# A two-layer decoder trunk on 8 cores: the mixer norm's weight applied behind the spatial product, and steps of the recurrent layer moved between engines

## The reference, cut to what matters

```
def rg_lru(xc, h0, w_a, b_a, w_x, b_x, lam):
    r = sigmoid(block_diag_linear(xc, w_a, b_a))
    i = sigmoid(block_diag_linear(xc, w_x, b_x))
    log_a = -LRU_C * r * softplus(-lam)
    a = exp(log_a)
    mult = sqrt(-expm1(2.0 * log_a))
    bterm = mult * (i * xf)
    ...
def lru_mixer(...):
    gate, xb = split(xn @ w_in)
    xc, conv_tail = causal_dwconv(xb, conv_past, conv_w, conv_b)
    h, h_last = rg_lru(xc, ...)
    y = (gelu(gate) * h) @ w_out
def gmlp_mixer(xn, w_in, ln_g, ln_b, w_s, b_s, w_out):
    u, v = split(gelu(xn @ w_in))
    v = layernorm(v, ln_g, ln_b)
    ws = where(mask, w_s, 0)              # (G, CHUNK, CHUNK), 8 groups, chunks of 128
    s = einsum('gts,bcsgd->bctgd', ws, vp) + b_s
    y = (u * s) @ w_out                   # v is returned too, for the samples
```

## Time and profile before

| | us |
|---|---|
| three runs: median | 1739.13 |
| three runs: lowest and highest | 1738.28 and 2018.64 |
| the profiled execution | 1739.17 |
| its span on the slowest core (core 5) | 1737.6 |
| spans of the 8 cores | 1728.8 to 1737.6 |
| mean granted clock of TensorE, by core | 0.988 to 0.992 |

### The profile page before, as it was taken

The page is one execution under the profiler, slowest core; times in us unless marked ns, Lnnn a source line. Parts: engine busy times, 40 slices in busy tenths (PEclk is TensorE's granted clock), DMA queues, the critical chain, the costliest instruction groups (busy, mean ns, idle before and its releaser), DMA issues.

```text
span 1737.6 us, 35664 instructions; the slowest of 8 cores (1728.8 to 1737.6 us)
## 1 busy us (share of the span) xinstructions
PE 1650.4 (95%) x10879; PEld 1052.6 (61%) x10879; DVE 1267.9 (73%) x2604; ACT 950.3 (55%) x1918; POOL 643.8 (37%) x1101
## 2 busy tenths in 40 slices
PE   5899989999999999999988999999999999999996
PEld 2566655666666666666544556656666666666655
DVE  4676666987767676777767877888776777677786
ACT  4877779644444444466655453864444444565756
POOL 1444447432111111136866654722111111254543
PEclk9899999999999999999999999999999999999998
DMA  8710040073212121210094000133440404001112
GB/s 158 169 56 2 2 79 1 3 133 69 44 31 48 27 49 25 43 20 1 11 164 79 2 1 1 27 63 66 78 73 2 74 1 74 2 5 38 39 48 101
DMA packets 24074, 82.96 MB, mean 48 GB/s; under 512 B 1872, under 2 KB 15504, under 8 KB 18128
## 3 DMA queue, kind: packets, MB, share of 16 engines
q0 software_dynamic: 9712, 59.16, 19.9%
q1 hardware_dynamic: 13200, 20.32, 3.5%
q10 hardware_dynamic: 976, 1.21, 0.3%
HBM read 129.81 MB, written 10.03 MB: 80 GB/s over the span
## 4 chain that ended last, share of the span: by engine, by line
PE 76%; DVE 7%; issue 5%; ACT 5%; POOL 4%; DMA 2%; DVEq 0%; ACTq 0%; POOLq 0%; SPq 0%
PE PS L583 76%; DVE SB L567 3%; POOL SB L542 3%; DVE SB L542 3%; ACT SB L531 2%; ACT L531 1%; DMA SB<-xT 1%; DVE SB L558 1%; ACT SB L572 1%; ACT PS L531 1%; DMA SB<-lru_w_a 0%; DMA SB<-lru_w_x_in 0%; POOL SB L558 0%; DVE SB L1363 0%; POOL SB L556 0%
## 5 line engine op out<-in xcount | busy, mean ns | idle before, releaser
L583 PE MATMUL PS<-SB 128*128 128x352 bf16 (+5 forms) x10879 | 1650.4, 313 | 79.3 <-ACT SB L531 36.2
L583 PEld LDWEIGHTS PS<-SB 128*128 128x128 bf16 x10879 | 1052.6, 98 | 676.9 <-issue 124.3
L567 DVE SCALAR_TENSOR_TENSOR SB<-SB 128x352 f32<-128x352 f32 (+1 forms) x708 | 398.0, 582 | 219.4 <-ACT SB L572 192.4
L542 POOL TENSOR_TENSOR SB<-SB 128x352 f32<-128x352 f32 (+12 forms) x457 | 437.1, 971 | 304.0 <-PE PS L583 103.2
L542 DVE TENSOR_TENSOR SB<-SB,PS 128x352 f32<-128x352 f32 (+3 forms) x960 | 458.2, 513 | 71.4 <-PE PS L583 54.0
L531 ACT ACTIVATE SB<-PS,SB 128x352 f32<-128x352 f32 (+1 forms) x432 | 256.7, 616 | 349.9 <-PE PS L583 336.1
L531 ACT ACTIVATE SB<-SB 128x352 f32<-128x352 f32 (+6 forms) x646 | 309.5, 505 | 236.5 <-DVE SB L567 136.4
L574 POOL COPY SB<-SB 128x2 f32<-128x2 f32 (+2 forms) x456 | 142.5, 317 | 623.3 <-ACT SB L572 446.9
L567 DVE SCALAR_TENSOR_TENSOR SB<-SB,PS 128x352 bf16<-128x352 f32 (+6 forms) x448 | 222.9, 546 | 92.6 <-ACT PS L531 50.1
L531 ACT ACT_TABLE_LOAD x111 | 142.4, 1283 | 56.3 <-PE PS L583 37.8
L572 ACT ACTIVATE SB<-PS 128x352 f32<-128x352 f32 (+7 forms) x408 | 159.8, 408 | 23.6 <-PE PS L583 12.2
(11 more groups left out here) (27 smaller groups left out, 55.8 us busy)
## 6 DMA issues: line engine op xcount, KB each, us to landing
SB<-ffn_w_up POOLq DMA_DIRECT2D x24, 1024.0 KB, 11.6
SB<-ffn_w_down POOLq DMA_DIRECT2D x12, 1024.0 KB, 9.1
SB<-xT SPq DMA_DIRECT2D x10, 704.0 KB, 9.0
yT<-SB SPq DMA_DIRECT2D x10, 704.0 KB, 3.3
SB<-ple_w_gate POOLq DMA_DIRECT2D x2, 2048.0 KB, 19.1
SB<-gm_w_in POOLq DMA_DIRECT2D x2, 2048.0 KB, 21.4
SB<-lru_w_x_in POOLq DMA_DIRECT2D x4, 512.0 KB, 10.5
SB<-lru_w_g_in POOLq DMA_DIRECT2D x2, 1024.0 KB, 19.8
```

The lines of the kernel that those rows point to most:

```text
L542: emit(eng, lambda e: e.tensor_tensor(out=out.ap, in0=a.ap, in1=b.ap, op=op), R=[a, b], W=[out], cost=c)
L567: emit("dve", lambda e: e.scalar_tensor_tensor(out=out.ap, in0=a.ap, scalar=sa, in1=b.ap, op0=op0, op1=op1), R=rr, W=[out], cost=c)
L583: emit("pe", lambda e: e.matmul(ps.ap, lhsT=lhsT.ap, rhs=rhs.ap, start=start, stop=stop), R=[lhsT, rhs], W=[ps], cost=max(0.05, 0.000427 * ...
```

## The change

The norm's weight and bias no longer touch v on its way to the spatial product. As the spatial product works on tokens and the weight stands per feature, the weight is applied behind it, as a scalar per partition in the same instruction that adds the position bias. The bias b of a feature becomes b times the row sum of the masked matrix; g_prep1 forms that with two products a group, of b in two bf16 parts, and adds it to bsB. Only the samples' block, whose v is an output, still gets both, in f32. The normalisation now writes the bf16 block itself.

In the recurrent layer: the load of lru_w_a waits for half a tile of x; tile 5's copies out of PSUM go from ACT to Vector; squares and clamps of tile 0 and of every other block of tile 5 go from Pool to Vector; tile 5's gates stand behind the exponentials and its roots behind the gates; two of the gates come with the output groups and six behind them. In layer 0's channel mixer the norms of tiles 2 to 5 form half of their squares on ACT, and lru_tail must be done before tile 3. `vecs` has 8 more columns.

```diff
+        lnbT = T(mem, [D], F32, off=ggate.off + 512)
+        lnbh = T(mem, [D], BF16, off=ggate.off + 4608)
+        lnbl = T(mem, [D], BF16, off=ggate.off + 6656)
...
-        load("pool", lw_a.all(), kp(w_la, KC), K("lwa"), hblock(0, 8, TN, TN))
+        load("pool", lw_a.all(), kp(w_la, KC), K("lwa"), hblock(0, 4, TN, TN))
...
-            cp(xb.v((3, 3 + npr)), sub(ps, 0, npr), eng="act")
+            cp(xb.v((3, 3 + npr)), sub(ps, 0, npr), eng="dve" if ns else "act")
             if ns:
-                cp(OLC.v(c, 0), sub(ps, npr - 3, npr), eng="act")
+                cp(OLC.v(c, 0), sub(ps, npr - 3, npr))
                 p3 = s4(sub(ps, npr, n))
                 cp(xs.v(None, (0, 3)), lcs.v(c), eng="pool")
-                cp(xs.v(None, (3, 7)), p3, eng="act")
-                cp(OLC.v(c, (1, 17)), V(p3.ap[:, :, 1:4], p3.bufs), eng="act")
+                cp(xs.v(None, (3, 7)), p3)
+                cp(OLC.v(c, (1, 17)), V(p3.ap[:, :, 1:4], p3.bufs))
...
-        def gate_group(ti, c):
+        def gate_group(ti, c, behind="sqrt"):
...
-            keep("gelu", act(gg[(ti + 1) % 2][c].v((0, n)), ps, AF.Gelu_apprx_tanh, order=phase("sqrt")))
+            keep("gelu", act(gg[(ti + 1) % 2][c].v((0, n)), ps, AF.Gelu_apprx_tanh, order=phase(behind)))
...
-            tt(m, a, a, ALU.mult, eng="pool")
-            ts(m, m, 1.0, ALU.min, 0.0, ALU.max, eng="pool")
+            eng = "dve" if ti == 0 or ti == 5 and c % 2 else "pool"
+            tt(m, a, a, ALU.mult, eng=eng)
+            ts(m, m, 1.0, ALU.min, 0.0, ALU.max, eng=eng)
...
-            keep("sqrt", act(m, m, AF.Sqrt, bias=0.25, scale=-0.25, order=phase("exp", "rstd")))
+            keep("sqrt", act(m, m, AF.Sqrt, bias=0.25, scale=-0.25, order=phase("gelu") if ti == 5 else phase("exp", "rstd")))
...
         for c in range(KC):
-            gate_group(5, c)
+            if c < 2:
+                gate_group(5, c, "exp")
             out_group(4, c)
+            tick()
+        for c in range(2, KC):
+            gate_group(5, c, "exp")
             tick()
...
-        bg.append(("xn2", xn_norm("nf0", 2, None, "pool", False)))
+        bg.append(("xn2", xn_norm("nf0", 2, None, ["act", "pool"] * 4, False)))
+        bg.append(("xn3", xn_norm("nf0", 3, None, ["act", "pool"] * 4, False)))
         bg.append(("tail", lru_tail()))
-        bg.append(("xn3", xn_norm("nf0", 3, None, "pool", False)))
-        bg.append(("xn4", xn_norm("nf0", 4, None, "pool", False)))
+        bg.append(("xn4", xn_norm("nf0", 4, None, ["act", "pool"] * 4, False)))
         bg.append(("out", lru_out()))
-        bg.append(("xn5", xn_norm("nf0", 5, None, "pool", False)))
+        bg.append(("xn5", xn_norm("nf0", 5, None, ["act", "pool"] * 4, False)))
...
                         if ti == 3:
+                            finish("tail")
                             load("sp", fcs.all(), st_fc[l].rearrange("p (c s k) -> p c s k", c=24, k=2), K("fcs"))
...
+            load("sp", lnbT.all(), lnb_d, K("lnbT"))
+            yield
+            cp(lnbh.all(), lnbT.all())
+            tt(lnbl.all(), lnbT.all(), lnbh.all(), ALU.subtract)
             yield
             for g in range(8):
                 tt(wsTm.v(g), wsTm.v(g), maskb.all(), ALU.mult)
                 tt(bd.v(g), bd.v(g), m64b.all(), ALU.mult)
                 yield
+                ps = BN(128)
+                mm(ps, lnbh.v((g * 128, (g + 1) * 128)), wsTm.v(g), True, False)
+                mm(ps, lnbl.v((g * 128, (g + 1) * 128)), wsTm.v(g), False, True)
+                tt(bsB.v(g), bsB.v(g), ps, ALU.add)
+                yield
...
-                ts(vbv, vbv, mv.v((0, 1), p=(0, nt)), ALU.subtract, mv.v((3, 4), p=(0, nt)), ALU.mult)
-                tt(vbv, vbv, lng.v(p=(0, nt)), ALU.mult)
                 vt = vT[i % 4]
+                ts(vt.v(p=(0, nt)), vbv, mv.v((0, 1), p=(0, nt)), ALU.subtract, mv.v((3, 4), p=(0, nt)), ALU.mult)
                 if smp:
+                    ts(vbv, vbv, mv.v((0, 1), p=(0, nt)), ALU.subtract, mv.v((3, 4), p=(0, nt)), ALU.mult)
+                    tt(vbv, vbv, lng.v(p=(0, nt)), ALU.mult, eng="pool")
                     tt(vbv, vbv, lnb.v(p=(0, nt)), ALU.add, eng="pool")
-                    cp(vt.v(p=(0, nt)), vbv, eng="act")
                     store("sp", o_v, vbv, K("ov"))
-                else:
-                    tt(vt.v(p=(0, nt)), vbv, lnb.v(p=(0, nt)), ALU.add, eng="pool")
...
+                gc = vcol("lng", g)
...
-                tt(s3, p3, V(bb.ap.unsqueeze(1).broadcast_to([128, nq, 128]), bb.bufs), ALU.add)
+                stt(s3, p3, gc, V(bb.ap.unsqueeze(1).broadcast_to([128, nq, 128]), bb.bufs), ALU.mult, ALU.add)
                 if ns:
                     b4 = bsB.v(g, (0, 4))
-                    tt(s4(sub(sv, npr, n)), s4(sub(pss, npr, n)), V(b4.ap.unsqueeze(1).broadcast_to([128, NSEQ, 4]), b4.bufs), ALU.add)
+                    stt(s4(sub(sv, npr, n)), s4(sub(pss, npr, n)), gc, V(b4.ap.unsqueeze(1).broadcast_to([128, NSEQ, 4]), b4.bufs),
+                        ALU.mult, ALU.add)
```

More of the change, by code:

```diff
@@ L413 @@
                ("lcw", 32), ("lcb", 8), ("ba", 8), ("bx", 8), ("lam", 8),
-               ("fcw0", 72), ("fcw1", 72), ("fcb0", 24), ("fcb1", 24)]:
+               ("fcw0", 72), ("fcw1", 72), ("fcb0", 24), ("fcb1", 24), ("lng", 8)]:
     VC[_n] = _o
@@ L1536 @@
         cols += [_chunks(f(ffn_conv_w)[l, j], 24) for j in range(3)]
-    cols += [_chunks(f(ffn_conv_b)[0], 24), _chunks(f(ffn_conv_b)[1], 24)]
+    cols += [_chunks(f(ffn_conv_b)[0], 24), _chunks(f(ffn_conv_b)[1], 24), _chunks(f(gm_ln_g)[0], 8)]
     vecs = np.ascontiguousarray(np.concatenate(cols, axis=1))
```

## The result

The changed kernel takes 1723.2 us (median; the runs beside it of the kernel before 1739.1). The ratio is 0.9908, 95% interval 0.9888 to 0.9927: 15.9 us less, within 2%. In one of its four executions, as in single executions of other kernels, the cores of one die ran at a lower clock and took longer; the ratios, and all times but this 1723.2, leave such executions out (after is then 1722.0). The profiled execution's slowest core has a span of 1722.9 us, the median core 1716.7 (before 1737.6 and 1734.4).

A forecast was written before the change was run, and what follows sets the result against it. PE was taken as the bound, idle only 87.2 of 1737.6 us, plus clock lost after waits. Terms 1.3 + 4.2 + 4.1 + 3.1 + 0 + 6.7 - 1.0 = 18.4 us off 1739.2 gave 1721; own range 1714 to 1728, overall 1707 to 1738.

The forecast's parts named there:

- Start: Kernel start: PE's 2.25 us wait for lru_w_a shrinks as its load needs half an x tile; gain 1.3 us.
- Tile 0: Recurrent layer, 58 to 69 us: squares and clamps on Vector bring ACT's roots sooner; gain 4.2 us, between 0 and 9.3.
- Tile 5, reads: Recurrent layer, 212 to 237 us: PSUM reads moved to Vector relieve ACT; gain 4.1 us, between 0 and 6.6.
- I take 8: Tile 5: Vector's cost for the 32 PSUM reads, 8 us, covered by its 12.78 us of idle time.
- Tile 5, gates: Recurrent layer, 285 to 325 us: PE keeps work in hand, fewer table changes; gain 3.1 us, between -4 and 6.2.
- Norms and tail: Layer 0's channel mixer: divided squares and the tail finished before tile 3 change nothing; 0 us.
- Preparation: Sixteen added 128-column products in PE's full stretch cost 1.0 us, 4 at most.
- gMLP: gMLP mixer: dropping a Vector product and a Pool sum per block cuts PE's waits; gain 6.7 us, between 0 and 10.7.
- gap of 957: gMLP: PE's longest wait for a draining add, 2.73 us before 957.04, was to be gone.
- A: Whole kernel: the waits only move and the gains halve, giving 1731 us; chance 0.25.
- B: Tiles 0 and 5: squares and clamps run 3.4 times slower on Vector beside Pool, giving 1728 us; chance 0.10.
- C: At 285 to 370 us Vector becomes the bound through added reads and pairs, giving 1747 us; chance 0.07.

The follow-up runs named there:

- e7_gates_as_before: e3_state_first with tile 5's gates and output groups taking turns and the old order of functions again; 1722.8 us, ratio 0.9911.
- e4_tail_as_before: The changed kernel with norms of tiles 2 to 5 and tail as in the kernel before (squares on Pool, tail not forced); 1717.0 us, ratio 0.9873.
- e3_state_first: The changed kernel with two of the next slice's three weight loads held until the small load st_fc has landed; 1715.7 us, ratio 0.9866.
- e5_tail_unforced: e3_state_first with the tail between the norms of tiles 2 and 3, not forced, squares still divided between ACT and Pool; 1716.5 us, ratio 0.9874.
- e2_layer0_only: The changed kernel without its gMLP part, so only the edits ahead of layer 0's channel mixer; 1733.0 us, ratio 0.9967.

## Why the prediction was right, and where it was not

The time of 1723.2 lies 2 us above the 1721 forecast and inside the forecast's own range, but the sum came out by errors that cancel, and that is luck. By the prediction's own last sentence the forecast fails as a whole if the gMLP gives over 12 us; it gave 12.4 by the time, with some 3 us of error, and 14 by the trace. Point by point:

- Start, 1.3: ahead by 1.3 us at the 136th product, 0.5 left at the end on the median core. Not told apart from the spread of the cores.
- Tile 0, 4.2: 3.4 on the median core, 5.0 over all executions. The mechanism was right: PE's waits at 55 to 72 us fell from 6.3 to 4.3 us, "a wait of some 3 us stays". The x tile was late for the issue of lru_w_out by 1.6 us, and nothing came of it.
- Tile 5, reads, 4.1: 7.4 to 8.5; after gains 6.2 us on before in this stretch. The term was mis-sized: "at most 2.8 of the 6.9 us come out at the end", taken from Pool's waits, was no bound. The whole wait of 3.87 us went, and the clock was worth 3.6 us over the stretch where I had looked at one window of 10 us and counted 1.7. The Vector side, "I take 8", measured 8.2, and ACT works 19.0 of 22 us at 215 to 237, before 21.3, as the prediction wanted.
- Tile 5, gates, 3.1: 3.7 to 5.2 on the median core when taken back, but over the kernel before the stretch that holds them, with the norms and the tail, gained 0.1 us. So the gain that the term stood for is not there; the edit keeps waits of PE for Vector (4.83 us in e7_gates_as_before) from coming, and these are not about table loads.
- Norms and tail, 0: this is the step that failed. It cost 6.1 us (e4_tail_as_before), 7.3 by the measure of e3_state_first alone, 6.0 at one place of the trace. "From 330 us on PE has no wait to give" says what PE can gain there, not what it can lose. Nor did I follow the queues behind the moved steps. Two edits that were both priced at nothing meet: `finish("tail")` puts st_fc at 348.73 us, where without it it goes out at 332.3 and 335.6 (e4_tail_as_before, e5_tail_unforced), and the squares taken from Pool let the weights out at 341.7 instead of 352.7. The second alone does no harm, as e5_tail_unforced shows.
- Preparation, 1.0: the lead falls by 0.9 us there.
- gMLP, 6.7: 12.4 us with the preparation taken out, 14 by the trace. It was mis-sized. The parts were valued by which of PE's waits named them, 3.5 for Pool and half of 6.4 for Vector, and then added. The runs show that they don't add: 0 and 0 alone, 14 to 15 together. The gap of 957 and the waits for Pool did go, as said.

The single experiments must not be added up: each was taken back inside the new kernel, and the four of the recurrent layer come to 0.5 + 3.4 + 7.4 + 3.7 = 15.0 us on the median core, where e2_layer0_only, with the 4.3 that st_fc cost it back, has 9.7. The lead of after over before can be added, stretch by stretch: 3.7 up to the 290th product (forecast 5.5), -0.4 to the 1152nd, 6.2 to the 1350th (4.1), 0.1 to the 2100th (3.1), -5.9 to the 2200th (0), -0.9 to the 4000th (-1.0), -0.7 to the 5700th, 14.1 to the 7200th (6.7). That makes 16.2, and the median core ends 17.7 us earlier. So +7.4 in the gMLP and +2.1 in the reads stand against -5.9 at st_fc and some -5 in the start and the gates. Without the loss at st_fc the kernel takes 1715.7 us, ratio 0.9866, the best version measured; e5_tail_unforced is its equal and shorter on the median core.

Of the rivals, A (waits only move) is true of the stretch from the 1350th to the 2100th product and of layer 0's mixer behind it; at tile 0, in the reads and in the gMLP the gains stayed. B falls: squares and clamps ran on Vector in 0.51 and 0.34 us. C named the right stretch, 285 to 370 us, and the wrong cause; Vector was busy 60.3 of 70 us at 300 to 370, less than before, and its reads cost nothing.

## What to carry to other kernels

When a step is forced earlier or finished by force, list every transfer issued behind it and what then goes out ahead of that transfer: a small load needed soon must leave before the large ones needed late, and small transfers in front of it on its own queue count too. Two instructions in a chain must not be valued one by one: if the chain has slack for one of them, each seems free and only the pair costs, so test a removal both singly and together. The same holds for gains: what an edit is worth when it is taken back from the new kernel is not what it added to the old one. And where cores start up to 6 us apart, compare the median core's trace beside the time.
